# Gate stage of a PEER layer taken in pairs of groups: 32-row comparison matmuls, two-bank VectorE steps, ScalarE on two tokens of eight

## The reference, cut to what matters

```python
best_s, best_pos = lax.top_k(cand_s, PEER_TOPK)          # per token and head: 16 experts
idx = jnp.take_along_axis(cand_i, best_pos, axis=-1)     # expert = row key * 128 + column key
gate = jax.nn.softmax(best_s, axis=-1)
act = jax.nn.gelu(einsum('nhkd,nd->nhk', expert_u[idx], xb))
return einsum('nhk,nhkd->nd', gate * act, expert_v[idx])
```

## Time and profile before

| | |
|---|---|
| median of 3 runs | 2294.34 us (2292.79 to 2294.65) |
| the profiled execution | 2293.73 us |
| its span, first to last instruction | 2291.9 us |
| busy share of PE, DVE, ACT, POOL | 94%, 51%, 46%, 58% |
| mean granted TensorE clock | 0.975 |
| gate stage of layer 0 | 739.39 to 825.90 us |
| gate stage of layer 1 | 1838.78 to 1925.3 us |

### The profile page before, as it was taken

One profiled execution on the slowest core, in us unless ns is written; L12 is line 12 of the kernel. 1 busy time (PEld: TensorE's weight loads), 2 busy tenths in 40 slices (PEclk: granted clock), 3 DMA queues, 4 the chain that ended last, 5 costly groups with the idle time before them and its releaser, 6 DMA issues.

```text
span 2291.9 us, 42131 instructions
## 1 busy us (share of the span) xinstructions
PE 2150.5 (94%) x14535; PEld 1978.5 (86%) x14562; DVE 1159.5 (51%) x1857; ACT 1063.1 (46%) x1535; POOL 1323.5 (58%) x648
## 2 busy tenths in 40 slices
PE   6878889999999999999988978999999999999998
PEld 6876889999999888888878968999999988888886
DVE  3988517992000974444434661599400088444444
ACT  3444345444544445555544434544454444555553
POOL 4660657998886035555548515798888802555552
PEclk9988999999999999999999979999999999999999
DMA  4440444555664046666544304455566503666663
GB/s 146 155 146 1 147 129 156 166 169 181 198 197 142 1 140 193 194 194 192 195 128 147 129 20 146 156 167 164 189 194 189 187 1 104 194 192 194 193 194 102
DMA packets 97707, 345.64 MB, mean 151 GB/s; under 512 B 10480, under 2 KB 14064, under 8 KB 97264
## 3 DMA queue, kind: packets, MB, share of 16 engines
q1 hardware_dynamic: 94512, 340.67, 46.8%
q10 hardware_dynamic: 3136, 4.19, 0.7%
HBM read 341.68 MB, written 3.15 MB: 150 GB/s over the span
## 4 chain that ended last, share of the span: by engine, by line
PE 55%; issue 23%; POOL 20%; DVE 1%; ACT 0%; POOLq 0%; another core or an unknown queue 0%; ACTq 0%; DVEq 0%
PE bank L998 30%; POOL wlo L392 20%; PE bank L697 17%; PE bank L977 5%; PE bank L965 2%; PE bank L737 0%; DVE big L1032 0%; POOLq L396 0%; POOLq L391 0%; ACT whi L438 0%; DVE rstd L1030 0%; DVE big L1470 0%; ACT hhi L656 0%; POOL hlo L426 0%; POOL big L410 0%
## 5 line engine op out<-in xcount | busy, mean ns | idle before, releaser
L392 POOL TENSOR_TENSOR wlo<-raw,whi 128x1024 fp32r<-128x1024 f32 x384 | 966.6, 2524 | 428.1 <-ACT whi L438 427.2
L697 PE MATMUL bank<-hhi,whi 128*128 128x256 f32 x3072 | 880.8, 287 | 76.2 <-DVE hlo L1042 33.7
L697 PE MATMUL bank<-hlo,whi 128*128 128x256 f32 x3072 | 875.9, 285 | 0.0
L697 PE MATMUL bank<-hhi,wlo 128*128 128x256 f32 x3072 | 875.5, 285 | 0.0
L438 ACT ACTIVATE whi<-raw 128x1024 fp32r<-128x1024 f32 x640 | 675.5, 1056 | 382.7 <-PE bank L998 333.5
L697 PEld LDWEIGHTS bank<-hhi,whi 128*128 128x128 f32 x3072 | 596.8, 194 | 84.1 <-issue 66.0
L426 POOL TENSOR_TENSOR hlo<-big,hhi 128x256 fp32r<-128x256 f32 x256 | 352.9, 1380 | 515.5 <-ACT hhi L661 515.5
L697 PEld LDWEIGHTS bank<-hlo,whi 128*128 128x128 f32 x3072 | 596.7, 194 | 0.1
L697 PEld LDWEIGHTS bank<-hhi,wlo 128*128 128x128 f32 x3072 | 596.4, 194 | 0.0
L1466 DVE TENSOR_TENSOR wlo<-raw,whi 128x1024 fp32r<-128x1024 f32 x256 | 316.8, 1239 | 367.0 <-ACT whi L438 366.9
L998 PE MATMUL bank<-whi,hhi 128*128 128x512 f32 x1024 | 315.5, 389 | 3.5 <-POOL hlo L426 3.5
(11 more groups left out here) (218 smaller groups left out, 1433.6 us busy)
## 6 DMA issues: line engine op xcount, KB each, us to landing
raw<-w_u SPq DMA_DIRECT2D x256, 512.0 KB, 3.4
raw<-w_v SPq DMA_DIRECT2D x256, 512.0 KB, 4.3
raw<-w_ssd_in SPq DMA_DIRECT2D x40, 512.0 KB, 3.5
raw<-w_q SPq DMA_DIRECT2D x32, 512.0 KB, 3.5
raw<-w_hgrn_in SPq DMA_DIRECT2D x32, 512.0 KB, 3.5
raw<-w_ssd_out SPq DMA_DIRECT2D x16, 512.0 KB, 3.5
raw<-w_hgrn_out SPq DMA_DIRECT2D x8, 512.0 KB, 3.6
big<-keys SPq DMA_DIRECT2D x2, 1024.0 KB, 6.3
```

The costliest lines, as they stand in the source:

```text
L392: nc.gpsimd.tensor_tensor(wlo[:, r, :, :], raw[:, r, :, :], whi[:, r, :, :].bitcast(F32), ALU.subtract).then_inc(lo_pool, 1)
L697: ins = nc.tensor.matmul(out, w[:, r, k, :], h[:, k, :], start=start and n == 0, stop=stop and n == 3 * KC - 1, **kw)
```

## The change

The stage is taken in 32 pairs m of groups, 8 tokens each. `feat_rows` is laid out so that each block of 32 partitions holds 4 tokens: blocks 0 and 1 side a, blocks 2 and 3 side b (two DMAs on ACT's queue in place of one, half the partitions each, the same elements). `matches(m)` becomes four bf16 matmuls of 32 rows, each with its own 32 partitions of weights and of moving data and its own bank (4 to 7). DVE's scalar_tensor_tensor covers 6 of the 8 tokens, over banks 6 and 7. ACT does the side b of the other 2 tokens with a Relu scaled by the gate, after its two Relus of side a, and signals it with a new semaphore `ohb_act`. `multiply` covers 8 tokens over two banks. There is one set of comparison banks instead of two, so `matches(m + 1)` now stands between the two halves of the L977 matmuls of pair m, behind waits for `oha_done` of the second half and `ohb_act`.

```diff
@@ -122,7 +122,8 @@
         small = sb("small", [P, 8, T])
         lbt = sb("lbt", [P, 6, KC])
         aexp = sb("aexp", [HEADS, 1])
-        bank = [ctx.enter_context(nc.psum_tensor(f"bank{i}", [P, 512], F32)) for i in range(8)]
+        banks = ctx.enter_context(nc.psum_tensor("banks", [P, 8, 512], F32))
+        bank = [banks[:, i, :] for i in range(8)]
         flat = big[:, :, :].rearrange("p a b -> p (a b)")
@@ -300,11 +302,11 @@
         oha = [hhi[:, 2 * r:2 * r + 2, :].rearrange("p a (b k) -> p (a b) k", k=P) for r in range(4)]
-        ohb = [raw[:, 2 + r // 2, 4 * (r % 2):4 * (r % 2) + 4, :] for r in range(4)]
+        ohb = [raw[:, 2 + r, :, :] for r in range(2)]
         whole = work(26112, 512, 4).bitcast(U32)
         feat = work(26624, 2048).bitcast(BF16).rearrange("p (c f k) -> p c f k", c=4, f=FEAT)
         feat_rows = small[:, :, :].rearrange("p a b -> p (a b)").bitcast(BF16) \
-            .rearrange("p (c s k) -> p c s k", c=4, s=8)
+            .rearrange("p (s k) -> p s k", s=32)
         feat_out_t = [nc.dram_tensor(f"feat{n}", [4, P, FEAT, P], BF16).ap() for n in range(2)]
         def level_bank(n, b):
@@ -361,7 +363,7 @@
                                 before = plo, pat[prev] + COUNT[prev] - RAW + r + 1
                             if name[0] == "v" and r == 2:
-                                sp.wait_ge(gate_mm, 64 * int(name[1]) + 64)
+                                sp.wait_ge(gate_mm, 32 * int(name[1]) + 32)
                         else:
                             before = lo, at[name] + RAW * i + r - RAW + 1
                         load(name, i, r, before)
@@ -642,24 +644,32 @@
                 act.wait_ge(lt_v, layer + 1)
                 act.wait_ge(feat_out, 16 * layer + 16)
-                act.dma_start(feat_rows, feat_out_t[layer].rearrange("c (s t) f k -> (t f) c s k", s=8)) \
-                    .then_inc(feat_in, 16)
+                for c in range(2):
+                    act.dma_start(feat_rows[64 * c:64 * c + 64], feat_out_t[layer][2 * c:2 * c + 2]
+                                  .rearrange("b (s t) f k -> (t f) (b s) k", t=8)).then_inc(feat_in, 16)
                 stream(f"u{layer}", gelu, 26)
-                for n in range(64):
-                    act.wait_ge(xa_mm, 64 * layer + n + 1)
-                    if n >= 4:
-                        act.wait_ge(gate_mm, 64 * layer + n - 3)
-                    nc.scalar.activation(oha[n % 4], bank[4 + n % 2][:, :].rearrange("p (n k) -> p n k", n=4),
-                                         ACT.Relu).then_inc(oha_done, 1)
+                for m in range(32):
+                    if m >= 2:
+                        act.wait_ge(gate_mm, 32 * layer + m - 1)
+                    for q in range(2):
+                        act.wait_ge(xa_mm, 64 * layer + 2 * m + q + 1)
+                        nc.scalar.activation(oha[2 * (m % 2) + q], bank[4 + q].rearrange("p (n k) -> p n k", n=4),
+                                             ACT.Relu).then_inc(oha_done, 1)
+                    act.wait_ge(ohb_done, 32 * layer + m + 1)
+                    for t in range(6, 8):
+                        a = 8 * m + t
+                        ins = nc.scalar.activation(ohb[m % 2][:, t, :], bank[7][:, P * (t - 4):P * (t - 3)],
+                                                   ACT.Relu, scale=gate_t[:, a:a + 1])
+                    ins.then_inc(ohb_act, 1)
                 def c_hi(j, r):
                     nc.scalar.activation(hhi[:, r, :], col(j), ACT.Copy).then_inc(chi, 1)
-                act.wait_ge(gated, 64 * layer + 64)
+                act.wait_ge(gated, 32 * layer + 32)
                 name = f"v{layer}"
                 c_hi(0, 0)
                 c_hi(1, 1)
@@ -957,28 +967,33 @@
                 pe.wait_ge(evac, EVAC[f"u{layer}"] + 128)
-                pe.wait_ge(feat_in, 16 * layer + 16)
-                def matches(n):
-                    for c, done in ((0, xa_mm), (1, xb_mm)):
-                        nc.tensor.matmul(bank[4 + 2 * c + n % 2][:, :], feat_rows[:, 2 * c + n // 32, n % 32 // 4, :],
-                                         signs[:, 4 * (n % 4):4 * (n % 4) + 4, :], start=True,
-                                         stop=True).then_inc(done, 1)
+                pe.wait_ge(feat_in, 32 * layer + 32)
+                def matches(m):
+                    for c in range(2):
+                        for q in range(2):
+                            u = 2 * c + q
+                            nc.tensor.matmul(bank[4 + u], feat_rows[32 * u:32 * u + 32, m, :],
+                                             signs[32 * u:32 * u + 32, 4 * u:4 * u + 4, :], start=True,
+                                             stop=True).then_inc((xa_mm, xb_mm)[c], 1)
                 matches(0)
-                matches(1)
-                for n in range(64):
-                    pe.wait_ge(oha_done, 64 * layer + n + 1)
-                    pe.wait_ge(ohb_done, 64 * layer + n + 1)
-                    if n >= 4:
-                        pe.wait_ge(gated, 64 * layer + n - 3)
-                    for t in range(4):
-                        ins = nc.tensor.matmul(bank[n % 4][:, P * t:P * (t + 1)], oha[n % 4][:, t, :].bitcast(F32),
-                                               ohb[n % 4][:, t, :], start=True, stop=True)
+                for m in range(32):
+                    pe.wait_ge(ohb_done, 32 * layer + m + 1)
+                    if m >= 2:
+                        pe.wait_ge(gated, 32 * layer + m - 1)
+                    for q in range(2):
+                        pe.wait_ge(oha_done, 64 * layer + 2 * m + q + 1)
+                        if q:
+                            pe.wait_ge(ohb_act, 32 * layer + m + 1)
+                            if m < 31:
+                                matches(m + 1)
+                        for t in range(4):
+                            ins = nc.tensor.matmul(bank[2 * (m % 2) + q][:, P * t:P * (t + 1)],
+                                                   oha[2 * (m % 2) + q][:, t, :].bitcast(F32),
+                                                   ohb[m % 2][:, 4 * q + t, :], start=True, stop=True)
                     ins.then_inc(gate_mm, 1)
-                    if n < 62:
-                        matches(n + 2)
                 pe.wait_ge(lt_v, layer + 1)
@@ -1437,26 +1452,27 @@
                 dve.wait_ge(lt_v, layer + 1)
-                def multiply(n):
-                    dve.wait_ge(gate_mm, 64 * layer + n + 1)
-                    v = big[:, :, 4 * n:4 * n + 4]
-                    nc.vector.tensor_tensor(v, v, bank[n % 4][:, :].rearrange("p (n j) -> p j n", n=4),
+                def multiply(m):
+                    dve.wait_ge(gate_mm, 32 * layer + m + 1)
+                    v = big[:, :, 8 * m:8 * m + 8]
+                    a = 2 * (m % 2)
+                    nc.vector.tensor_tensor(v, v, banks[:, a:a + 2, :].rearrange("p a (n j) -> p j (a n)", n=4),
                                             ALU.mult).then_inc(gated, 1)
                 dve.wait_ge(evac, EVAC[f"u{layer}"] + 128)
-                for n in range(64):
-                    dve.wait_ge(xb_mm, 64 * layer + n + 1)
-                    if n >= 4:
-                        dve.wait_ge(gate_mm, 64 * layer + n - 3)
+                for m in range(32):
+                    dve.wait_ge(xb_mm, 64 * layer + 2 * m + 2)
+                    if m >= 2:
+                        dve.wait_ge(gate_mm, 32 * layer + m - 1)
                     nc.vector.scalar_tensor_tensor(
-                        out=ohb[n % 4], in0=bank[6 + n % 2][:, :].rearrange("p (n k) -> p n k", n=4), scalar=0.0,
-                        in1=gate_t[:, 4 * n:4 * n + 4].unsqueeze(2).to_broadcast([P, 4, P]), op0=ALU.is_gt,
+                        out=ohb[m % 2][:, 0:6, :],
+                        in0=banks[:, 6:8, :].rearrange("p a (n k) -> p (a n) k", n=4)[:, 0:6, :], scalar=0.0,
+                        in1=gate_t[:, 8 * m:8 * m + 6].unsqueeze(2).to_broadcast([P, 6, P]), op0=ALU.is_gt,
                         op1=ALU.mult).then_inc(ohb_done, 1)
-                    if n >= 2:
-                        multiply(n - 2)
-                multiply(62)
-                multiply(63)
+                    if m:
+                        multiply(m - 1)
+                multiply(31)
                 name = f"v{layer}"
```

More of the change, by code:

```diff
@@ L232, in trunk @@
         ohb_done = sem("ohb_done")
+        ohb_act = sem("ohb_act")
         xa_mm = sem("xa_mm")
```

## The result

The changed kernel takes 2301.46 us (median of 7 runs, 2299.18 to 2302.06), the kernel before 2293.74 (7 runs): a ratio of 1.0033, 95% interval 1.0021 to 1.0044. The forecast was 2296.0, with a range from 2286 to 2306. The time lies in the range, but the profile shows that the road there was another than the one I had added up.

What follows compares the result with a forecast made beforehand. The prediction took the gate stage's wait loop through one set of comparison banks as the bound: 0.48 + 0.95 + 0.12 + 1.00 + 0.11 = 2.66 us a turn, +1.7 us over two stages, forecast 2296.0 us, range 2286 to 2306.

Steps and rivals of the forecast that it cites:

- the way around: Gate stage: comparison, L1452 (now L1468), first half of L977, next comparison wait on each other; 2.66 us, above any engine's sum.
- The turn: Gate stage: one pair of groups takes 2.66 us, what two groups took before; bounds 2.42 and 3.03.
- PE's own sum: Gate stage: PE's work per pair, 2.36 us; rival that it sets the pace, 2277 us, chance 4 in 100.
- the first term: Gate stage turn: start of comparison to start of L1452 (now L1468), 0.43 plus 0.05 stagger, 0.48 us.
- PE's restart: Gate stage turn: from the end of L1452 (now L1468) to PE's first weight load, 0.12 us.
- The stagger: Gate stage: spread of the four comparison matmuls' starts from three short weight loads, 0.05 us, bounds 0 and 0.33.
- Side by side: Gate stage: the four 32-row comparison matmuls run at once; rival that they don't, 2333 us, chance 10 in 100.
- ACT's part and `multiply`: Gate stage: ACT's two extra Relus (about 0.28 us each) and `multiply` (1.21 us, 0.38 to spare) stay hidden.
- "The feature DMAs: [...] so nothing": Stage `u`: one more issue on ACT's queue, landing over 40 us ahead of its use, costs nothing.
- "The longer last step is in the sum [...] queue behind it as they do now": Gate stage's end: last `multiply` of 1.21 us, before 0.68, is counted; ACT, POOL and PE of stage `v` queue behind unchanged.
- The forecast's +1.7: Both gate stages together: each 87.3 us instead of 86.5, so the kernel gets 1.7 us slower.
- The rival that gives 2302: Gate stage: signals take longer with four matmuls signalling separately, turn 2.75 us, +7.3 us; chance 26 in 100.

Runs made afterwards that it cites:

- experiment 3: Changed kernel with each of the four comparison matmuls over all 128 rows instead of 32: 2325.96 us (one run).
- 4: Changed kernel with one signal for the four comparison matmuls in place of four: 2293.43 us, ratio 1.0009 to the kernel before.
- 8: Changed kernel with the later second feature DMA and side b of all 8 tokens on DVE, none on ACT: 2313.88 us (one run).
- experiment 6: Changed kernel with later second feature DMA, one comparison signal, and the next pair's comparisons issued ahead of both halves: 2278.16 us, ratio 0.9942.
- experiments 1: Changed kernel with the second feature DMA issued 8 tiles of stage `u` later on ACT's queue: 2292.82 us, ratio 1.0005 to the kernel before.
- experiment 5: Kernel before with its one feature DMA split into two, issued one behind the other on ACT's queue: 2297.37 us, ratio 1.0023.
- experiments 2: Changed kernel with the zero matmuls at the gate stage's end issued three times over: 2297.96 us, ratio 1.0019 to the kernel before.
- 7: Kernel of experiment 6 with the zero matmuls at the stage's end issued three times over: 2277.46 us, ratio 0.9941 to the kernel before.
- Experiment 9: Changed kernel with the second feature DMA 8 tiles later and four ACT copies in its old place: 2297.06 us, ratio 1.0021 to the kernel before.
- 10: Kernel before with four ACT copies added behind its one feature DMA: 2293.98 us, ratio 1.0005.

## Why the prediction was right in its time and where it failed

- **What bounds the stage, and the way around: right.** The turn was forecast at 2.66 and is 2.63. Term by term, forecast and measured (760.40 to 763.03): comparison to L1468 0.48 and 0.52; L1468 0.95 and 0.96; to PE's load 0.12 and 0.05; load, half and change of shape 1.11 and 1.10. In experiments 3, 4 and 8 the turn moved by what the changed terms moved, within 0.01 us, and in 6 it fell to PE's own sum once the halves were out of the way around. That the sum comes so near is partly luck: the first term was 0.04 too small and PE's restart 0.07 too large. The first term holds two errors itself. The stagger is 0.01, not 0.05, so the Trainium skill's page that the prediction weighed ("TensorE: Matmul & The Clock Gate", Part 3, with its 4 ns between starts) was nearer than the row. And three more signals cost 0.08, which I had as a rival and not in the sum. With 0.01, the 0.08 and a restart of 0.05 the same sum gives 2.63.
- **Side by side: right**, shown by experiment 3. **ACT's part and `multiply`: right** as hidden. A Relu of 128 elements with a scale took 0.36 instead of 0.28, within the margin.
- **"The feature DMAs: [...] so nothing": this step failed.** I priced the transfer's landing, which is hidden, and not the issue on ACT's queue, though ACT has work for every tile of stage `u`. The two issues hold ACT for 2.14 us where its idle time is 1.55. That is 1.04 + 0.92 = 2.0 us, shown by experiments 1 and 5.
- **"The longer last step is in the sum [...] queue behind it as they do now": half of it, and this step failed too.** The 0.53 us are in it, but they also lengthen PE's idle time from 1.72 to 2.26, and at that length the clock fell in 10 of 14 cases, 1.6 us each. That keeping PE busy there removes the fall is shown by experiments 2 and 7; that the longer `multiply` is what made it begin is argued from the counts of idle times. I had read 1.00 for the clock in both gate stages and never asked what keeps it there.
- **The loss of 7.7 us** in the two profiles is then 2.0 from the issues, 3.2 from half-clock stretches in `v`, 1.2 from one in the second gate stage, and 2.7 from more of them between the layers, less 1.2 at the beginning of the kernel, which the change doesn't touch, and 0.1 in the gate stage of layer 0.
- **The forecast's +1.7** came from the stage (4.88 + 31 x 2.66), and that was 0. The range to 2306 was made for a longer turn; the time lies in it through costs that the prediction had put at nothing, so that it holds is luck. The rival that gives 2302 came nearest in time, but its mechanism costs 2.4 us a stage inside a turn that is as long as before. The agreement of its number with the result is chance.

**What stays open.** The part between the layers takes 282.6 to 283.1 us with 41.0 us at half clock (before, 1, 3, 4, 6, 8, 9, 10), 284.8 to 285.7 with 47.8 (changed, 5, 7) and 286.9 with 54.6 (2). Its work is the same in all of them. Why the longer stretches come in some kernels and not in others is not settled, nor why the clock fell at the beginning of the second gate stage in the changed kernel and in 2 alone. Experiment 9 points to small shifts in time, but I can't say which shift brings them.

## What to carry to other kernels

Making each engine's work cheaper gained nothing here, as the same edit gave up the distance between them: with one set of buffers add up the way around, and try to move the step that refills the buffer ahead of the long work, as in experiment 6 (-0.58% with the edits of 1 and 4). A DMA costs its queue the issue, not only the landing: look at what that queue feeds in those 2 us. And where a change makes the last step of a stage longer, look at how long PE then idles and whether the clock holds.

## What the runs showed of the hardware

- Four matmuls of 32 rows and 512 columns took 0.39 us together, against 1.03 for four full ones. Their starts lie within 0.01 us.
- A change between full and 32-row tiles cost 0.10 us in the stream too (1.10 us from the load to the next comparison, against 1.00 in experiment 3, which has no such change).
- Four signals from matmuls that end together delay the waiter by 0.08 us against one (0.52 and 0.44).
- Two DMA issues in a row on ACT's queue took 2.14 us (2.61 in experiment 5), one alone 0.59 to 0.82.
- DVE read across two banks at the cost of its elements: 0.957 us for 768, 1.22 for 1024.
